# Head passes two and a half slots apart, what follows three slots later, and three steps of choice up to slot 63, in a two-layer block kernel

## The reference

```
x  = x + gt1 * (mixed @ w_out)                      # mixed: 8 forgetting heads, 8 stick-breaking heads
h2 = rms_norm(x) * (1 + sc2) + sh2
query = h2 @ w_query                                # 8 heads x 2 halves x 128
sub_scores = einsum(query, sub_keys)                # 128 keys for each half
half_vals, half_idx = top_k(sub_scores, 16)
cand = half_vals[0][:, None] + half_vals[1][None]   # 16 x 16
top_vals, top_pos = top_k(cand, 16)                 # 16 experts for each token and head
act = gelu(einsum('td,thkd->thk', h2, expert_down[experts])) * softmax(top_vals)
x  = x + gt2 * einsum('thk,thkd->td', act, expert_up[experts])
```

## Time and profile before

| | |
|---|---|
| median of three runs | 1505.47 us |
| the profiled execution | 1501.87 us |
| its span | 1500.1 us |
| TensorE, VectorE, ScalarE, GpSimd busy | 89%, 72%, 36%, 26% |
| read from HBM | 431 MB, of which the gathers 268 MB |
| first gather issued, last dot begun | 193.1 us, 864.9 us |

### The profile page before, as it was taken

How to read it: one execution, slowest core, us unless ns; L and a number is a source line. 1 busy time by engine, 2 the same in 40 slices (tenths; PEclk the granted TensorE clock), 3 DMA queues, 4 the chain that set the end, 5 groups by cost and what they waited for, 6 DMA issues and landing times.

```text
span 1500.1 us, 17348 instructions
## 1 busy us (share of the span) xinstructions
PE 1340.0 (89%) x6338; PEld 944.7 (63%) x6338; DVE 1078.5 (72%) x2034; ACT 534.6 (36%) x1040; POOL 394.3 (26%) x337
## 2 busy tenths in 40 slices
PE   6999989799998777777877799999999999999997
PEld 6887565356554323233323258879888788798896
DVE  6777789767897888888555576587656679876664
ACT  3453245422222212213211154535434355454440
POOL 1100034444444544454443202101101043011110
PEclk9999999999999999999999999999999999999999
DMA  9757589999999999999999994345554443455440
GB/s 364 281 200 265 183 342 394 402 421 416 420 421 406 421 421 421 422 410 406 408 422 422 402 333 151 113 146 194 179 211 172 172 158 123 148 203 210 169 169 28
DMA packets 116692, 433.17 MB, mean 289 GB/s; under 512 B 6896, under 2 KB 7152, under 8 KB 83584
## 3 DMA queue, kind: packets, MB, share of 16 engines
q0 software_dynamic: 36864, 268.45, 43.5%
q1 hardware_dynamic: 79456, 162.51, 30.5%
q10 hardware_dynamic: 288, 1.11, 0.2%
HBM read 431.00 MB, written 1.05 MB: 288 GB/s over the span
## 4 chain that ended last, share of the span: by engine, by line
PE 55%; DMA 21%; DVE 15%; ACT 5%; issue 2%; POOL 2%; SPq 0%; DVEq 0%; ACTq 0%; POOLq 0%
PE PS L1577 34%; DMA EB<-in_experts,EI 19%; PE PS L1804 4%; DVE EB L2666 4%; PE PS L1805 4%; PE PS L1560 3%; PE PS L1779 2%; PE PS L1573 1%; PE PS L1558 1%; DMA W<-in_w_out 1%; DVE WL L2333 1%; POOL EB L2945 1%; PE PS L1637 1%; PE PS L1819 1%; ACT BIG L2144 1%
## 5 line engine op out<-in xcount | busy, mean ns | idle before, releaser
L2945 POOL DMA_INDIRECT EB<-in_experts,EI x256 | 300.4, 1174 | 494.1 <-PE PS L1805 310.0
L2666 DVE CUSTOM_DVE_ANT_0 EB<-EB,Y 128x1024 f32<-128x1024 f32 x256 | 313.0, 1224 | 117.2 <-DMA EB<-in_experts,EI 116.5
L1804 PE MATMUL PS<-EB,BIG 128*128 128x512 f32 x512 | 279.0, 627 | 117.1 <-ACT BIG L2144 116.9
L2333 DVE TENSOR_TENSOR WL<-W,WH 128x1024 fp32r<-128x1024 f32 x216 | 279.8, 1344 | 88.6 <-ACT WH L1962 86.1
L1805 PE MATMUL PS<-EB,BIG 128*128 128x512 f32 x512 | 267.6, 605 | 0.0
L1804 PEld LDWEIGHTS PS<-EB,BIG 128*128 128x128 f32 x512 | 90.6, 195 | 252.4 <-ACT BIG L2144 182.6
L1962 ACT ACTIVATE WH<-W 128x1024 fp32r<-128x1024 f32 x216 | 213.4, 1048 | 71.3 <-PE PS L1573 67.6
L1577 PE MATMUL PS<-XH,WH 128*128 128x256 f32 x736 | 212.2, 288 | 0.6 <-ACT BIG L2188 0.6
L1577 PE MATMUL PS<-XL,WH 128*128 128x256 f32 x736 | 207.4, 282 | 0.0
L1577 PE MATMUL PS<-XH,WL 128*128 128x256 f32 x640 | 180.5, 282 | 0.0
L1805 PEld LDWEIGHTS PS<-EB,BIG 128*128 128x128 f32 x512 | 99.9, 195 | 127.2 <-issue 127.2
(11 more groups left out here) (353 smaller groups left out, 1818.8 us busy)
## 6 DMA issues: line engine op xcount, KB each, us to landing
W<-in_ffn_w SPq DMA_DIRECT2D x32, 2048.0 KB, 8.8
W<-in_w_ada SPq DMA_DIRECT2D x11, 2048.0 KB, 10.6
W<-in_hy_w_in SPq DMA_DIRECT2D x6, 2048.0 KB, 11.4
W<-in_gla_w_in SPq DMA_DIRECT2D x6, 2048.0 KB, 8.1
W<-in_w_in SPq DMA_DIRECT2D x5, 2048.0 KB, 14.2
W<-in_w_out SPq DMA_DIRECT2D x2, 2048.0 KB, 13.4
W<-in_w_query SPq DMA_DIRECT2D x2, 2048.0 KB, 21.6
W<-in_w_query SPq DMA_DIRECT2D x4, 1024.0 KB, 6.8
```

Source lines behind the costliest of these rows:

```text
L1804: e.matmul(PS[u[0][0]][:, :], DG[i], rows_up[:, 1024:1536], start=start, stop=stop)
L2333: e.tensor_tensor(tile.lo[:, k, :], tile.w[:, k, :], tile.hi[:, k, :].bitcast(F32), ALU.subtract).then_inc(*VE.up(("lo", tile.index, n)))
L2666: e.tensor_tensor_reduce(out=u, in0=u, in1=Y[:, s // 128, :], scale=1.0, scalar=0.0, op0=ALU.mult, op1=ALU.add, accum_out=dots[:, s:s + 1] ...
L2945: e.indirect_dma_start(out=EBUF[i], out_offset=None, in_=A["experts"][:, :], in_offset=bass.IndirectOffsetOnAxis(ap=EI[:, t, j:j + 1], axi ...
```

## The change

The eleven passes of the heads that lie in the loop are at slots 0, 2, 5, 7, 10, 12, 15, 17, 20, 22, 24, where they were at 0, 2, 4 up to 20. Everything that follows them, from the square of their norm to x1's copy, is three slots later. The query products of head group 2 begin at slot 42 where they began at 40, and end with the copy of scores at slot 48 where that was at 47. Those of the second tile's group 0 begin at slot 49, where that was 48, and end at 55 as before. Slots 49 to 63 call three steps of choice each, where they called two, and three at each fourth. `JOIN` and the waits of the gathers are as they were.

```diff
-            for i in range(11):
-                beside[2 * i].append(lambda: next(heads))
-            for n, steps in ((24, (head_square,)), (25, (first,)), (26, (second, lambda: turned(bank()))),
-                             (28, (copy, lambda: wout_rest(0, 1))), (30, (lambda: wout_rest(1, 1), lambda: do.load_query(2))),
-                             (31, (lambda: piece(0),)), (33, (lambda: piece(1),)), (34, (x1_first,)), (35, (x1_second, x1_turn)),
-                             (37, (x1_copy,))):
+            for n in (0, 2, 5, 7, 10, 12, 15, 17, 20, 22, 24):
+                beside[n].append(lambda: next(heads))
+            for n, steps in ((27, (head_square,)), (28, (first,)), (29, (second, lambda: turned(bank()))),
+                             (31, (copy, lambda: wout_rest(0, 1))), (33, (lambda: wout_rest(1, 1), lambda: do.load_query(2))),
+                             (34, (lambda: piece(0),)), (36, (lambda: piece(1),)), (37, (x1_first,)), (38, (x1_second, x1_turn)),
+                             (40, (x1_copy,))):
                 beside[n] += steps
             for n in (0, 1, 3):
                 beside[n].append(lambda: next(second_query))
-            for t, j, at_slots in ((0, 2, (40, 41, 42, 43, 45, 46, 47)), (1, 0, (48, 49, 50, 51, 53, 54, 55)),
+            for t, j, at_slots in ((0, 2, (42, 43, 44, 45, 46, 47, 48)), (1, 0, (49, 50, 51, 52, 53, 54, 55)),
...
-                for _ in range(3 if s < 32 or 73 <= s < 92 or s % 4 == 3 else 2):
+                for _ in range(3 if s < 32 or 49 <= s < 64 or 73 <= s < 92 or s % 4 == 3 else 2):
```

## The result

The changed kernel takes **1521.04 us** (median of 5 runs, 1519.29 to 1522.55), beside 1504.87 us for the kernel before (5 runs, 1503.46 to 1506.13): a ratio of 1.0109, 95% interval 1.0098 to 1.0120, or 16.2 us more. The forecast was 1511.5, with a range up to 1515.0. The direction was right, and the size is 10 us short. The profiled execution took 1519.93 us, with a span of 1518.1: 18.0 us more than the profiled execution before. Of these, 15.4 us are there at the last dot. The other 2.6 lie in the layers behind the slots. That part takes 635 to 638 us in all the traces here, so such a difference between single executions says nothing about the change.

The account below looks back on a forecast made before the run. It took the slots to be bound by DMA. +7.3 (late buffer) - 0.7 (made up) - 0.6 (choice) = +6.0 us, on 1505.47, gave 1511.5 us, range 1507.5 to 1515.0.

Parts of the forecast that it names:

- Part 1: Head passes spread over 24 slots for 20: faster pace early, gather 26 late; +7.3 us at gather 31, 0.7 made up.
- late buffer: Buffer 7, freed only by the last pass at slot 24: gather 26 issued at 269.2, gather 31 landing 7.3 us late.
- Part 2: Norm, w_out's rest, w_query load and x1 three slots later, keeping their distances from each other: cost 0.
- pace gain: Slots 2 to 15: pairs relieved of an even-slot pass run faster, slot 23's up 1.9 us earlier (bounds 0 to 2.9).
- The clock: Rival: TensorE's low clock behind the stall holds gathers 34 to 37 back up to 3.8 us, 1515.3 us; chance 0.07.
- What comes back: Gathers 31 to 40, after the stall: 0.7 us of the loss made up (bounds 0 to 1.4).
- Part 3: Choice, three steps in slots 49 to 63: gather 96's wait for expert numbers goes, 0.6 us won (bounds 0 to 1.0).
- Covered buffer: Rival: gather 26 issued before about 262, so only the gains are left, 1502.5 us; chance 0.09.
- half-covered buffer: Rival, no change: TensorE reaches the last pass some 4 us sooner, leaving +0.9 us, 1506.4 us; chance 0.10.
- the lateness of about 6 us at slot 40 isn't there at the end: Sign that the forecast is wrong: the delay expected at slot 40 would be gone by the end.

Follow-up runs that it names:

- a2: Changed kernel with buffer 7 joining the ring at slot 30 in place of 26: 1510.07 us, ratio 1.0032.
- d4: a2 with the query's copy, its scores and their copy one slot later, at slots 47, 48, 49: 1505.25 us, ratio 1.0002.
- a3: Changed kernel with no step of choice at slot 49: 1514.17 us, ratio 1.0067.
- b2: Kernel before with only the query products of slots 42 to 55 moved as in the change: 1508.92 us, ratio 1.0025.
- b3: Kernel before with the norm, w_out's rest, the w_query load and x1 three slots later, query at its old slots: 1512.53 us, ratio 1.0050.
- b1: Kernel before with three steps of choice in slots 49 to 63 and nothing else changed: 1503.86 us, ratio 0.9990.
- d3: Kernel before with query products moved as in the change, but the query's copy, scores and their copy at 47, 48, 49; two steps of choice: 1511.52 us.
- e2: Changed kernel with head passes back at every even slot and the query's copy, scores and their copy at slots 47, 48, 49: 1507.00 us, ratio 1.0016.
- a4: Kernel before with the head passes alone at the new slots, 0 to 24: 1511.67 us, ratio 1.0039.

## Why the prediction was right and wrong

**In short.** The forecast was +6.0 us and the kernel lost 16.2. Two steps failed. Part 1's cost was mis-sized: 6.6 us (+7.3 - 0.7) were forecast for the late buffer, and 11 to 11.6 measured (changed kernel to a2). Part 2 was put at 0 and measured 4.5 (a2 to d4).

**The mechanism of part 1's cost was right.** Gather 26 behind the last pass, gathers 27 to 31 right behind it, DMA dry: all of it is in the trace, and a2 shows that it is the larger loss. The size was off. The forecast had +7.3 at the landing of gather 31 and +6.6 at slot 40. The trace has gather 26 at 13.6 us later for the 9.5 of the forecast, dot 31 at 9.2 and dot 40 at 9.8. Three terms of the working failed:

- *The pace gain, 1.9 us, isn't there.* The premise was that a pass at an odd slot puts its exponential and table loads off the chain. ScalarE's and VectorE's share of the chain that ended last, from slot 5's gate (L2673) to slot 9's, shows them on it:

```profile
218.02 0.16 DVE BIG L2673
...
223.42 0.17 DVE BIG L2673
...
223.62 0.69 ACT BIG L2144 x2
224.33 1.28 ACT L2062
225.62 0.56 ACT BIG L2062 x2
...
226.85 1.28 ACT L2138
228.14 0.21 ACT BIG L2138
...
228.38 0.16 DVE BIG L2673
```

  ScalarE is at work from the diagonal matrices behind slot 7's gate (223.62) to slot 9's gelu (228.14) without a break, with the pass of slot 7 in between. So pair 8-9, with no pass of its own, takes 228.38 - 223.42 = 4.96 us for the 4.36 of the forecast. In pair 6-7 VectorE works from gate to gate: 223.42 - 218.02 = 5.40, where I had worked out 4.6 from its average and put the pair at 4.76. The pace before wasn't 5.21 throughout either, since that was one pair. By the gates the four relieved pairs (4-5, 6-7, 8-9, 14-15) took 5.13, 5.49, 4.81 and 5.22 before and take 4.38, 5.40, 4.96 and 4.77 now: 1.1 us won for the 2.2 of the forecast. Behind them 0.6 is lost again, in pairs 16-17 (5.56 for 5.31) and 18-19 (5.90 for 5.58). The maximum of the pass at slot 15 falls behind that slot's gate, so two maxima move into these pairs, where the forecast counted one. From slot 1's gate to slot 23's it is 58.4 us for 59.0 before. This execution began its slots 1.0 us later, so nothing of that is left at 267.19.
- *The clock, left out of the forecast and given 0.07 as a rival.* The low level came earlier than the rival had it, in the ups just ahead of the last pass: 272.42 - 267.19 = 5.23 us for four pairs of matmuls, where the spacing of the earlier trace rows gives 3.56, so 1.7 us. With the 1.9 of the pace and the 0.4 of a later start this makes up the 4.0 us from 269.2 to 273.25. Another execution can differ, since the clock isn't the same in each: a3 is the same program up to slot 49, TensorE was idle for the same 2.81 us, and it ran the burst at full clock, in 3.53 us for the 3.56 of the spacing:

```profile
266.99 1.12 PE L1804 MATMUL PS<-EB,BIG 128*128 128x512 f32 x2 [2.81 <-ACT BIG L2144]
267.95 1.02 PE L1805 MATMUL PS<-EB,BIG 128*128 128x512 f32 x2
```

  The Trainium skill ("TensorE: Matmul & The Clock Gate", section "HAM oscillation — how this bites in real kernels") says that waits for DMA throttle the array, and that the next work starts cold. Ahead of the last pass the wait was one for ScalarE, and the trace doesn't agree there: the first pair ran in 1.12 us and the fall came after it, and in a3 and in the kernel before (3.19 us idle) it didn't come. Behind the stall the trace agrees: after 7.88 us idle the first pair, at 284.34, takes 2.08 us. That is the rival's own place. The clock is 0.56 there (280 to 290) with DMA at 1.01, and what it costs can't be told apart.
- *What comes back, 0.7 us by slot 40.* Nothing did: dot 31 is 9.2 and dot 40 is 9.8 us later.

**Part 2 at 0 was the step whose mechanism failed.** I looked at where the norm, the load and x1 would stand, and passed over the query's slots altogether, but for x1's copy ahead of slot 49. Moving products from 40-43 to 42-45 and the copy from 45 to 46 takes away the free slot and turns an odd slot into an even one, with a gelu behind the copy for one ahead of it. a2 to d4 measures 4.5 us for it. (b2, 3.8 us, holds a later choice as well.) Who stands behind a moved step on its own engine was asked of GpSimd and SyncE, not of ScalarE. The wq2 load was looked at and wrongly passed: "nine slots to land as it had ten" took the landing time for fixed, while its median grew from 11.1 to 18.0 us (b3), 18.7 in the changed kernel. In the change itself the query's later start hides that, as argued, by luck rather than by the right number.

**Part 3 was right.** In the changed kernel gather 96 waits for TensorE, no more for a choice:

```profile
464.76 1.25 POOL L2945 DMA_INDIRECT EB<-in_experts,EI  x1 [2.56 <-PE PS L1805]
```

The 0.6 us taken for it and the 1.5 of b1 agree within b1's interval. d3 points to what the extra steps are for: without them the later query costs 6.5 us, with gathers 64 and 96 late. d3 with the three steps wasn't run.

**The rivals.** Covered buffer and half-covered buffer are refuted: TensorE reached the pass at 272.42, not by 262, and no sooner than I said. What would make me wrong, "the lateness of about 6 us at slot 40 isn't there at the end", pointed the wrong way: it grew to 15.4.

**What stays open:** why single executions run this burst at one clock or the other; how much of b3's loss is the load's and not the norm's; why e2 is 2.4 us over the kernel before while d4, with the same wait for weights, is level with it; and why a4 costs only 5.9 us with a gap as long as the one for which a2 gives 11. As early as gather 7, where most of these programs don't differ yet, single traces lie 1 to 4 us behind the kernel before, which bounds what offsets can tell.

## What to carry to other kernels

When a step moves by a slot, list what stands directly behind it on **its own** engine, and where its input stands in the queue of the engine that makes it: a short copy that waits for a product at the end of a busy TensorE's queue holds up all that follows it, and a slot of distance or the other side of the gelu is worth some 4.5 us here (a2 to d4). When a shared ring waits for a one-time user (buffer 7 for the last pass), move the joining point together with that user; the wait of one gather stops all gathers behind it. Time a weight load by what is in the other queue when it is issued, and not by how long the same load took elsewhere; and take the pace of a stretch from its pairs one by one, not from an engine's average.

## What the hardware showed that was not expected

- TensorE's clock fell within a burst, and not in every execution. Four kernels have the same work and the same 2.81 us of idle time ahead of the ups of slots 22 and 23. Their four pairs of matmuls took 1.12, 1.73, 1.92 and 1.21 us in the changed kernel, 2.07, 1.91, 1.92 and 1.34 in a2, 1.34, 1.91, 1.70 and 1.02 in a4, and 1.12 and three times 1.02 in a3. The burst differs by up to 2.9 us by that, which no count of instructions shows.
- The same two loads of 1 MB land in 7.7 and 14.4 us in the kernel before and in 15.6 and 20.4 in b3, with more gathers under way in the other queue.
- A large hole in DMA doesn't close: dots 50 to 255 keep a lateness of 14.2 to 19.4 us over 500 us, with DMA's share at 1.00 to 1.02 from 370 on. What looks like a denser pace, 421 GB/s from 520 to 865 for 413 before, isn't one: those are other slots, and from 535 to 880, where the changed kernel does about what the other did from 520 to 865, it moves 415 GB/s. A small one can close: in d4 dot 55 is 2.9 us late, and the last dot is on time.
